# Two reorders on ScalarE and VectorE, and four large weight copies issued three tiles apart instead of at one place

## The chip, the cores and the metric

The kernel runs on one core of a Trainium2 chip. TensorE (PE in the rows) multiplies, ScalarE (ACT), VectorE (DVE) and GpSimd (POOL) do the rest, and SyncE (SP) issues most of the DMAs; GpSimd issues some. Each engine works through its own queue in order and waits on semaphores. The metric is the device time of one execution in microseconds (us). It was 1953.87 us, the median of 3 runs (1952.58 to 1955.76). A difference of under 0.2%, some 3.9 us, is about what a measurement can't tell from none.

## The reference, cut to what matters

One decoder layer for 1024 tokens and 16 meta tokens, width 1024, in float32:

```
proj = rmsnorm(h) @ w_in                      # 80 blocks of 128 columns, and 16 gate columns
gq, gk, gv = silu(causal_dwconv(...))         # 4 taps
y_a = gated_delta(gq, gk, gv, ...)            # chunked recurrence, 8 heads
y_b = retention(rotary(rq), rotary(rk), rv)   # chunked recurrence, 4 heads
h = h + (sigmoid(gate_a) * y_a + sigmoid(gate_b) * y_b) @ w_out
u = causal_dwconv(rmsnorm(h) @ w_ffn_up, 3 taps) + bias
a, b = split(u)
h = h + (silu(a) * b) @ w_ffn_down
out = rmsnorm(h)
```

## The kernel before, in words

All large products are made of three matrix products each: an operand x is split into a rounded high part and a remainder, and PE sums high x high, high x low and low x high. ACT makes the high part of a weight block (`split_high`, L1550), DVE the low part (`split_low`, L1941).

**The plan.** Up to the end of the input projection, every engine walks the same list of steps, which `front_plan` writes. A tile t is a block of 128 columns of `w_in`, and it is computed in three thirds (t, 0), (t, 1), (t, 2) of its some 1040 rows (step `proj`, L1171). Two banks of PSUM take turns, so PE starts a third only when ACT has copied out the third before the last one (`evac`, ACT L1625). The weights of tile t+2 are loaded when tile t+1 has been split (step `load`, L844), and split beside tile t+1. Tiles 0 to 15 are the rotary ones: DVE rotates a pair of tiles (`rope`, L2006 to L2016), SP stores it. Tiles 15 and 16 are computed in one piece (`proj3`, L155). Beside tile 15, ACT and DVE write the input anew, scaled by its norm, into `xh` and `xl` (ACT L1635, DVE L2028, 8 blocks each). Tile 17 needs its own low part in `w_lo`, which stands in DVE's queue behind the rope of tiles 14 and 15. Tiles 16 to 23 and 32 to 47 go through a convolution on DVE (step `conv`, L2049 and L2053) and then SiLU on ACT (step `silu`, L1684). Between the thirds stand the steps of the two recurrences. `dec` (DVE L2163, L2166) and `dec_e` (ACT L1724, L1726: two exponentials) prepare the decay factors of a chunk. The list writes SiLU of tile 46 after the third (47, 1). From tile 48 on the helper `fill` adds the thirds. A table of ACT's functions is loaded (ACT_TABLE_LOAD) whenever SiLU, exponential or sigmoid follow each other.

**The four weight copies.** For the last product (`w_ffn_down`) sums of its quarters are needed. GpSimd copies four quarters, 2816 KB each, from memory to memory as the starting values of these sums (L2589, queue q0), when tile 4 is done; later it adds to them by DMA.

**The up projection.** The first three column pairs of `w_ffn_up` are done plainly. The other 19 (pair i, i = 0 to 18, j = i + 3) are each made of seven products of half size, in PE's order 0 to 6 (pair 0 in another order), L1470. Products 0, 1, 2 and 3 go into four regions of PSUM, which are then reused: product 4 adds to the region of product 0, product 5 to that of product 2, product 6 to that of product 3. DVE's `combine(i, n)` for n = 0 to 4 (L2425, L2427, L2429, L2431, L2433) puts the regions together. PE starts product 5 of pair i only after `combine(i, 1)`, which reads product 2, and product 6 only after `combine(i, 2)`, which reads product 3. Between these, DVE does for pair j-1 the convolution (`taps`, L2361), the product with the SiLU (`gate_product`, L2367) and sums for the last product (`act_sums`: one operation up to j-1 = 10, three from 11 on, L2377 to L2383). For pair i+1 it makes four sums of weights (`quarter_sum`, L2332) and seven low parts (`quarter_split`, L2338), whose high parts ACT makes (L1789).

**Names in the rows.** `post` are the seven row buffers; `w_raw`, `w_hi`, `w_lo` a block of weights and its parts; `up_*` the same for the up projection; `u_one`, `u_two`, `u_three` the results in the combining.

Of the kernel before, what the change touches and what calls it, by code (L numbers as in the profile page):

```python
# [178 lines left out]
def front_plan():  # L179

    plan = []
    add = plan.append
# [8 lines left out]
    def unit(t, j):  # L191
        add(("proj", t, j))
        if j == 0 and not T_RV - 1 <= t < T_Q - 1 and t != T_ZB - 1:
            add(("split", t + 1))
        for n in splits_at.get((t, j), ()):
            add(("split", n))
# [26 lines left out]
    steps = {u: [] for u in range(96)}  # L223
# [11 lines left out]
    u = 34  # L235
    for b in range(NBATCH):
# [3 lines left out]
        j = 0  # L240
        while j < B32 - 1:
            u += 1
            n = min(B32 - 1 - j, 2 if u < 49 or u % 2 else 3)
# [21 lines left out]
    steps[91] += [("dl_k", 0), ("expand", 0)]  # L265
    steps[92] += [("dec", 0), ("dec_e", 0), ("qk", 0), ("dl_g", 1), ("dl_m", 1), ("dl_x", 1)]
    steps[93] += [("dl_a", 1)]
    steps[94] += [("dec", 1), ("dec_e", 1)]
    steps[95] += [("tk", 0), ("expand", 1), ("dl_x", 2)]

    def conv_tile(t):
        return T_K <= t < T_RV or T_Q <= t < T_ZB

    for u in range(96):
        t, j = T_K + u // 3, u % 3
        if t > T_K:
            unit(t, j)
        elif j == 0:
            add(("split", t + 1))
            add(("proj3", t))  # L280
            weights(t, 0)
            add(("rturn", 7))
        if j == 1 and conv_tile(t - 1):
            add(("silu", t - 1))
        if u in (90, 93):
            weights(t, j)
            add(("vstore", t - 2))
        for step in sorted(steps[u], key=lambda step: step[0] in ("tin", "tout")):
            add(step)
        if u in (92, 95):  # L290
            add(("split", T_ZB + u // 95))
        if j == 2 and (T_K <= t - 1 < T_RV or T_V <= t - 1):
            add(("vturn" if T_V <= t - 1 else "kturn", t - 1))
            if u not in (89, 92):
                add(("vstore" if T_V <= t - 1 else "kstore", t - 1))
        if t > T_K and u not in (90, 93):
            weights(t, j)
        if not conv_tile(t):
            add(("rvstore", 3 * t + j))
        elif j == 2:  # L300
            add(("conv", t))
# [4 lines left out]
    def fill():  # L306
        due, early = list(splits), list(ahead)
        splits.clear()
        ahead.clear()
        while held:  # L310
            add(held.pop(0))
        while gates:
            add(("gate", gates[-1]))
            splits.append(gates.pop())
        for n in early:
            add(("oload", n))
        t, j = units.pop(0)
        add(("proj", t, j))
        if j == 0:
            held.extend((*((("split", t + 1),) if t > T_ZB else ()), ("load", t + 2)))  # L320
        for n in due:
            if n >= 8:
                add(("ysplit", n))
            if n < 15:
                ahead.append(n + 1)
        if j == 2 and (t - T_ZB) % 2:
            add(("sig", (t - T_ZB) // 2))
            gates.append((t - T_ZB) // 2)

    fill()  # L330
    fill()
    add(("silu", T_ZB - 1))
    add(("vturn", T_ZB - 1))
# [6 lines left out]
    for c in range(NCH):  # L340
        n, nn = c + 1 < NCH, c + 2 < NCH
# [77 lines left out]
def program(nc, io, sc, out):  # L419

    with ExitStack() as ctx:
# [10 lines left out]
        def sem(name):  # L432
            return ctx.enter_context(nc.semaphore("f1_" + name))
# [113 lines left out]
        def w_parts(t):  # L547
# [4 lines left out]
            if 6 <= n < 8:  # L552
# [30 lines left out]
               for n in range(2)]  # L583
# [7 lines left out]
        w_hi, w_lo, units_done, evac, pe_x15 = (sem(n) for n in (  # L591
            "w_hi", "w_lo", "units_done", "evac", "pe_x15"))
# [16 lines left out]
        d_dec, a_dec, a_eg, w_sums, pe_qk, d_attn, pe_lev, d_q5, d_x5, d_t6, a_q6, d_x6 = (  # L609
            sem(n) for n in ("d_dec", "a_dec", "a_eg", "w_sums", "pe_qk", "d_attn", "pe_lev", "d_q5", "d_x5", "d_t6",  # L610
                             "a_q6", "d_x6"))
# [177 lines left out]
        def tiles_done(t):  # L789
            return 3 * t + 3  # L790
# [1144 lines left out]
        def _(dve):  # L1935
# [25 lines left out]
            for step in plan:  # L1961
                kind, a = step[0], step[1:]
# [32 lines left out]
                elif kind == "rope":  # L1995
                    i = a[0]
# [33 lines left out]
                elif kind == "rturn":  # L2030
                    i = a[0]
# [5 lines left out]
                elif kind == "conv":  # L2037
                    t = a[0]
                    q = convs_before(t)
                    tile = t - T_K + 8 if t < T_RV else t - T_Q if t < T_V else t - T_V + 16  # L2040
                    n = T - FRONT
# [126 lines left out]
                elif kind == "qk":  # L2168
                    c = a[0]
                    dve.wait_ge(a_dec, c + 1)  # L2170
                    for g in range(2):
                        dve.wait_ge(pe_qk, 2 * c + g + 1)
                        into = at[c % 2][seen(c), heads(g), seen(c)]
# [7 lines left out]
                elif kind == "l5r":  # L2181
                    c = a[0]
                    dve.wait_ge(pe_lev, lev(c, 2))
                    for n in range(2):
                        for odd in range(2):
                            of = 64 * odd + B32 * n
# [15 lines left out]
                elif kind == "kturn":  # L2202
                    t = a[0]
                    n = t - T_K
# [7 lines left out]
                elif kind == "vturn":  # L2212
                    t = a[0]
                    n = t - T_V
# [72 lines left out]
                elif kind == "gate":  # L2287
                    n = a[0]
# [75 lines left out]
            def gate_product(j):  # L2364
                dve.wait_ge(silu, j + 1)
                dve.wait_ge(conv, 4 * j + 4)
                dve.tensor_tensor(acc_of(j, 0), acc_of(j, 0), acc_of(j, 1), ALU.mult).then_inc(prod, 1)  # L2367
# [44 lines left out]
            def combine(i, n):  # L2412

                j = J0 + i
                left, right = slice(0, H2), slice(H2, 2 * H2)
                one, two, three = (x[:, :] for x in (u_one, u_two, u_three))
                dve.wait_ge(pe_p, max(made(i, m) for m in ((0, 1), (1, 2), (1, 2, 3), (5,), (6,))[n]))
                if n in (1, 2, 3, 4):
                    dve.wait_ge(comb, 5 * i + (None, 1, 2, 1, 1)[n])
                if n > 1:  # L2420
                    dve.wait_ge(conv, 4 * (j - 1) + (None, None, 4, 2, 4)[n])
                    dve.wait_ge(tap0, 2 * (j - 1) + (None, None, 2, 1, 2)[n])
                if n == 0:
                    dve.wait_ge(c11, 2 * i + 1)
                    ins = dve.tensor_tensor(two, region(i, 1), one, ALU.subtract)  # L2425
                elif n == 1:
                    ins = dve.tensor_tensor(three, two, region(i, 2), ALU.subtract)  # L2427
                elif n == 2:
                    ins = dve.tensor_tensor(u_out[1][:, right], three, region(i, 3), ALU.subtract)  # L2429
                elif n == 3:  # L2430
                    ins = dve.tensor_tensor(u_out[0][:, right], region(i, 2), two, ALU.subtract)  # L2431
                else:
                    ins = dve.tensor_tensor(u_out[1][:, left], two, region(i, 3), ALU.subtract)  # L2433
                ins.then_inc(comb, 1)
# [50 lines left out]
            for i in range(NPAIR):  # L2485
                j, more = J0 + i, i + 1 < NPAIR
                if i:
                    combine(i - 1, 4)
                    taps(j - 1, 0)
                    taps(j - 1, 1)  # L2490
                    combine(i, 0)
                    gate_product(j - 1)
                    act_sums(j - 1)
                if more:
                    quarter_sum(i + 1, 0)
                    quarter_sum(i + 1, 1)
                if i:
                    combine(i, 1)
                if more:
                    quarter_sum(i + 1, 2)  # L2500
                    quarter_sum(i + 1, 3)
                    quarter_split(i + 1, 0)
                    quarter_split(i + 1, 1)
                if i == 0:
                    gate_product(J0 - 1)
                    act_sums(J0 - 1)
                if not more:
                    for q in range(DEARLY):
                        down_low(q)
                if i:  # L2510
                    combine(i, 2)
                if more:
                    for n in range(2, 6):
                        quarter_split(i + 1, n)
                combine(i, 3)
                if more:
                    quarter_split(i + 1, 6)
# [57 lines left out]
        def _(pool):  # L2575
            pool.memset(zero, 0.0).then_inc(zero_set, 1)
            wd, rows = io["w_ffn_down"][0], KH * P
            a11, a12, a21, a22 = (wd[rows * k:rows * k + rows, 512 * m:512 * m + 512] for m in range(2) for k in range(2))
            ws = [sc["ws"][n].rearrange("k p c -> (k p) c") for n in range(4)]
# [3 lines left out]

            for step in plan:
                kind, a = step[0], step[1:]
                if kind == "proj" and a == (5, 0):
                    pool.wait_ge(units_done, tiles_done(4))
                    for into, of in zip(ws, (a21, a11, a11, a12)):
                        pool.dma_start(into, of).then_inc(w_sums, 16)  # L2589
                elif kind == "proj" and a[0] >= T_ZA and (3 * (a[0] - T_ZA) + a[1]) % 2 and 3 * (a[0] - T_ZA) + a[1] < 4 * KH:  # L2590
                    k = (3 * (a[0] - T_ZA) + a[1]) // 2
                    pool.wait_ge(units_done, 3 * a[0] + a[1])
                    pool.wait_ge(w_sums, 64)
                    n, k, of = (0, k, a22) if k < KH else (2, k - KH, a21)
                    add_block(n, k, of[k * P:k * P + P, :])
# [84 lines left out]
            for j in range(FT):  # L2680
# [3 lines left out]
                n, k = (1, 3)[j // KH], j % KH  # L2684
# [88 lines left out]
```

## Time and profile before

| What | Value |
|---|---|
| Median of 3 runs | 1953.87 us |
| Profiled execution: its own time, its span | 1952.47 us, 1950.7 us |
| PE busy | 1926.2 us (99%), 13173 matmuls |
| PE weight loads busy | 1859.4 us (95%) |
| DVE, ACT, POOL busy | 1283.4 us (66%), 795.9 us (41%), 328.8 us (17%) |
| DMA | 315.99 MB, mean 162 GB/s |
| Chain that ended last | PE 90%, DVE 5% |

By stages (from the span's start):

| Stage | us | PE busy | PE clock | DMA share |
|---|---|---|---|---|
| tiles 0 to 16 | 0 to 207 | 197.47 of 207 | 1.00 | 0.68 |
| tiles 17 to 47, retention | 207 to 687 | 479.74 of 480 | 1.00 | 0.59 |
| turn from tile 47 to tile 49 | 687 to 705 | 12.96 of 18 | 0.91 | 0.80 |
| rest of the input projection, gated delta, start of w_out | 705 to 1210 | 504.60 of 505 | 1.00 | 0.52 |
| w_out, first plain pairs | 1210 to 1341 | 131.00 of 131 | 1.00 | 0.29 |
| up projection in seven products | 1341 to 1727 | 383.88 of 386 | 1.00 | 0.44 |
| down projection | 1727 to 1951 | 216.56 of 224 | 0.99 | 0.65 |

PE is busy nearly throughout, so a time is lost or won only where PE stands still or its clock is lower. Idle time of the others costs nothing by itself. PE clock 1.00 is full speed (2.4 GHz), 0.50 is half of it (1.2 GHz).

### The profile page before, as it was taken

The page shows a single profiled execution, that of the slowest core. Times are in us where ns is not written, and L with a number is a line of the kernel's source. Part 1 is how long each engine was busy: PE and PEld are TensorE (multiplying, and loading weights), DVE is VectorE, ACT ScalarE, POOL GpSimd, SP SyncE. Part 2 cuts the span into 40 slices and gives each one's busy share as a digit, 9 for nine tenths or more (in the row PEclk, how much of TensorE's full clock was granted, in tenths as well). Part 3 has the DMA queues.
Part 4 walks back from the last instruction along what each step waited for, and adds up shares of the span by engine and source line. Part 5 has one row for each costly group of instructions (what it writes and reads, how often), then busy time and mean ns, then how long its engine had stood idle before and what let it go on. Part 6 is the DMA issues. An engine that isn't in the chain of part 4 may idle for free.

```text
span 1950.7 us, 32138 instructions
## 1 busy us (share of the span) xinstructions
PE 1926.2 (99%) x13173; PEld 1859.4 (95%) x13173; DVE 1283.4 (66%) x1612; ACT 795.9 (41%) x1094; POOL 328.8 (17%) x327
## 2 busy tenths in 40 slices
PE   8999999999999989999999999999999999999998
PEld 7999997999999989999999999999999999988887
DVE  6456764647676767667644434379988889877656
ACT  5223432534333445445443333235444344445443
POOL 0000002566573122212201010200000000000001
PEclk9999999999999999999999999999999999999999
DMA  9665566654455675555535552312433545578554
GB/s 296 227 203 140 129 167 190 201 181 161 156 185 141 155 179 175 164 162 153 166 108 158 157 155 77 106 68 82 131 100 109 152 152 162 152 259 280 192 191 158
DMA packets 301222, 315.99 MB, mean 162 GB/s; under 512 B 151004, under 2 KB 221124, under 8 KB 300948
## 3 DMA queue, kind: packets, MB, share of 16 engines
q1 hardware_dynamic: 291860, 290.86, 47.9%
q0 software_dynamic: 9216, 23.07, 5.8%
q8 instruction: 105, 1.72, 0.4%
q14 instruction: 41, 0.34, 0.0%
HBM read 222.76 MB, written 114.18 MB: 173 GB/s over the span
## 4 chain that ended last, share of the span: by engine, by line
PE 90%; DVE 5%; issue 1%; ACT 1%; DMA 1%; POOL 1%; DVEq 0%; SPq 0%; ACTq 0%; POOLq 0%
PE a_psum L1171 37%; PE a_psum L1470 18%; PE a_psum L1480 11%; PE a_psum L155 7%; PE a_psum L1158 5%; PE a_psum L1258 1%; PE a_psum L1277 1%; DVE post L2361 1%; PE a_psum L1255 1%; PE a_psum L1363 1%; PE a_psum L1287 1%; PE a_psum L1347 1%; PE a_psum L1378 1%; PE a_psum L1303 1%; PE a_psum L1386 1%
## 5 line engine op out<-in xcount | busy, mean ns | idle before, releaser
L1171 PE MATMUL a_psum<-xh,w_hi 128*128 128x342 f32 (+3 forms) x1632 | 529.0, 324 | 5.0 <-ACT post L1625 5.0
L1171 PE MATMUL a_psum<-xl,w_hi 128*128 128x342 f32 (+3 forms) x1632 | 523.9, 321 | 0.0
L1171 PE MATMUL a_psum<-xh,w_lo 128*128 128x342 f32 (+3 forms) x1632 | 522.0, 320 | 0.0
L1171 PEld LDWEIGHTS a_psum<-xh,w_hi 128*128 128x128 f32 x1632 | 307.7, 189 | 7.4 <-ACT post L1625 5.3
L1171 PEld LDWEIGHTS a_psum<-xl,w_hi 128*128 128x128 f32 x1632 | 307.9, 189 | 0.8
L1171 PEld LDWEIGHTS a_psum<-xh,w_lo 128*128 128x128 f32 x1632 | 307.7, 189 | 0.0
L1625 ACT ACTIVATE post<-a_psum 128x342 f32<-128x342 f32 (+3 forms) x204 | 93.2, 457 | 498.1 <-PE a_psum L1171 467.1
L1941 DVE TENSOR_TENSOR w_lo<-w_raw,w_hi 128x1024 fp32r<-128x1024 f32 x86 | 113.3, 1318 | 129.9 <-ACT w_hi L1550 129.9
L1550 ACT ACTIVATE w_hi<-w_raw 128x1024 fp32r<-128x1024 f32 x86 | 90.5, 1053 | 90.9 <-PE a_psum L155 62.6
L1480 PE MATMUL a_psum<-act_hi,down_hi 128*128 128x512 f32 (+1 forms) x324 | 124.4, 384 | 0.0
L1480 PE MATMUL a_psum<-act_hi,down_lo 128*128 128x512 f32 (+1 forms) x324 | 123.3, 381 | 0.0
L1470 PE MATMUL a_psum<-x_t_hi,up_hi 128*128 128x256 f32 x608 | 122.8, 283 | 0.3 <-DVE post L2429 0.2
L1470 PE MATMUL a_psum<-x_part_lo,up_hi 128*128 128x256 f32 x608 | 122.5, 283 | 0.0
L1480 PE MATMUL a_psum<-act_lo,down_hi 128*128 128x512 f32 (+1 forms) x324 | 122.5, 378 | 0.0
L2361 DVE SCALAR_TENSOR_TENSOR post<-post,c_par,post 128x1024 f32<-128x1024 f32 x88 | 111.2, 1282 | 2.4 <-ACT post L1826 0.6
L2053 DVE SCALAR_TENSOR_TENSOR post<-post,a_par,post 128x1040 f32<-128x1040 f32 x72 | 96.9, 1346 | 2.6
L1470 PEld LDWEIGHTS a_psum<-x_t_hi,up_hi 128*128 128x128 f32 x608 | 94.3, 190 | 0.6 <-issue 0.6
L1470 PEld LDWEIGHTS a_psum<-x_part_lo,up_hi 128*128 128x128 f32 x608 | 94.3, 189 | 0.0
L1470 PE MATMUL a_psum<-x_b_hi,up_hi 128*128 128x256 f32 x456 | 92.0, 283 | 1.9 <-DVE u_three L2427 1.7
L2582 POOL DMA_DIRECT2D down_sums<-down_sums x22 | 17.9, 814 | 444.1 <-DVE post L2367 444.1
L1470 PE MATMUL a_psum<-x_t_hi,up_sum_lo 128*128 128x256 f32 x456 | 91.8, 283 | 0.0
L1470 PE MATMUL a_psum<-x_t_lo,up_hi 128*128 128x256 f32 x456 | 91.5, 282 | 0.0
(294 smaller groups left out, 3947.3 us busy)
## 6 DMA issues: line engine op xcount, KB each, us to landing
w_raw<-in_w_in SPq DMA_DIRECT2D x75, 512.0 KB, 3.8
up_raw<-in_w_up SPq DMA_DIRECT2D x19, 1024.0 KB, 4.8
mix_scratch<-post SPq DMA_DIRECT2D x32, 522.0 KB, 3.0
down_sums<-in_w_ffn_down POOLq DMA_DIRECT2D x4, 2816.0 KB, 28.6
act_scratch<-post SPq DMA_DIRECT2D x22, 512.0 KB, 2.7
down_raw<-down_sums SPq DMA_DIRECT2D x44, 256.0 KB, 2.7
act_raw<-act_sums SPq DMA_DIRECT2D x44, 256.0 KB, 3.0
ext<-mix_scratch SPq DMA_DIRECT2D x9, 1024.0 KB, 7.2
```

The costliest lines, as they stand in the source:

```text
L155: mm = pe.matmul(psum[:, bank + j, 0:n], w[:, k, :], x[:, k, col + n * j:col + n * j + n], start=(k == 0 and part == 0), stop=(k == KC - 1 ...
L1158: mm = pe.matmul(psum[0:rows_, u % 2, n * i:n * i + n], x[:, k, x0:x0 + rows_], w, start=(k == 0 and part == 0), stop=(k == KC - 1 and par ...
L1171: mm = pe.matmul(psum[:, u % 2, 0:n], w[:, k, :], x[:, k, at0:at0 + n], start=(k == 0 and part == 0), stop=(k == KC - 1 and part == 2))
L1255: mm = pe.matmul(o, rvs[c % 2][seen(c), n, :], rsc[seen(c), h, seen(c)], start=True, stop=(c == 0))
L1258: mm = pe.matmul(o, rS[:, h, i, e * P:e * P + P], rqd[:, 2 * h + i, :], start=False, stop=(i == 1))
L1470: mm = pe.matmul(region(i, n)[:, piece], w[:, k, :], x[:, k, piece], start=(n < 4 and k == 0 and part == 0), stop=(k == 3 and part == 2), ...
L1480: mm = pe.matmul(psum[:, (0, 4, 0, 4, 0, 4, 0)[p] + m, c0:c0 + n], a, b[:, c0:c0 + n], start=(p not in (2, 5, 6) and k == 0 and part == 0) ...
L1550: act.activation(w_parts(t)[0], wr(t), ACT.Copy).then_inc(w_hi, 1)
L1625: act.activation(dst, src, ACT.Copy).then_inc(evac, 1)
L1941: dve.tensor_tensor(lo, wr(t), hi.bitcast(F32), ALU.subtract).then_inc(w_lo, 1)
L2053: dve.scalar_tensor_tensor(out=acc[:, 0:n], in0=x, scalar=w, in1=acc[:, 0:n], op0=ALU.mult, op1=ALU.add).then_inc(d_conv, 1)
L2361: dve.scalar_tensor_tensor(out=acc_of(j, s), in0=u_out[s][:, c0:c0 + SEQ], scalar=par2[:, at0:at0 + 1], in1=acc_of(j, s), op0=ALU.mult, op ...
```

## The change

It has three parts. PE and SP carry out the same instructions in the same order as before.

1. In the plan, `silu` of tile 46 stands after the third (47, 2) and not after (47, 1), and the exponentials `dec_e(1)` stand after the third (48, 0) and not before (47, 2).
2. In the up projection, `combine(i, 1)` of pairs 1 to 18 follows right behind `combine(i, 0)`, ahead of `gate_product`, `act_sums` and the first two sums of weights.
3. GpSimd issues the four copies one by one, when tiles 4, 7, 10 and 13 are done, and not all when tile 4 is done.

```diff
@@ front_plan
-    steps[94] += [("dec", 1), ("dec_e", 1)]
+    steps[94] += [("dec", 1)]
...
-        if j == 1 and conv_tile(t - 1):
+        if u == 95 or (j == 1 and u != 94 and conv_tile(t - 1)):
             add(("silu", t - 1))
...
     fill()
+    add(("dec_e", 1))
     fill()
     add(("silu", T_ZB - 1))
@@ VectorE, up projection
                     combine(i, 0)
+                    combine(i, 1)
                     gate_product(j - 1)
                     act_sums(j - 1)
                 if more:
                     quarter_sum(i + 1, 0)
                     quarter_sum(i + 1, 1)
-                if i:
-                    combine(i, 1)
@@ GpSimd
-                if kind == "proj" and a == (5, 0):
-                    pool.wait_ge(units_done, tiles_done(4))
-                    for into, of in zip(ws, (a21, a11, a11, a12)):
-                        pool.dma_start(into, of).then_inc(w_sums, 16)
+                if kind == "proj" and a[1] == 0 and a[0] in (5, 8, 11, 14):
+                    pool.wait_ge(units_done, tiles_done(a[0] - 1))
+                    n = (a[0] - 5) // 3
+                    pool.dma_start(ws[n], (a21, a11, a11, a12)[n]).then_inc(w_sums, 16)
```

ACT's queue before, from the copying out of the third (47, 0) on. The row of `post_57` is the SiLU of tile 46, the two `y` rows are `dec_e(1)`, and `w_hi` is the high part of tile 49.

```order
L1625 ACTIVATE post_55<-a_psum 128x348
L1625 ACTIVATE post_55<-a_psum 128x346
L1534 ACT_TABLE_LOAD
L1684 ACTIVATE post_57<-post_56 128x1040
L1534 ACT_TABLE_LOAD
L1724 ACTIVATE y<-y 128x1024
L1726 ACTIVATE y<-y 128x1024
L1625 ACTIVATE post_55<-a_psum 128x346
L1550 ACTIVATE w_hi<-w_raw 128x1024
L1625 ACTIVATE post_54<-a_psum 128x342 x2
L1534 ACT_TABLE_LOAD
L1684 ACTIVATE post_58<-post_56 128x1040
```

The same place in the changed kernel (its lines are one higher); the last row is followed by the SiLU of tile 47, as before.

```order
L1626 ACTIVATE post_55<-a_psum 128x348
L1626 ACTIVATE post_55<-a_psum 128x346 x2
L1535 ACT_TABLE_LOAD
L1685 ACTIVATE post_57<-post_56 128x1040
L1551 ACTIVATE w_hi<-w_raw 128x1024
L1626 ACTIVATE post_54<-a_psum 128x342
L1535 ACT_TABLE_LOAD
L1725 ACTIVATE y<-y 128x1024
L1727 ACTIVATE y<-y 128x1024
L1626 ACTIVATE post_54<-a_psum 128x342
L1535 ACT_TABLE_LOAD
```

The copying out of the third (47, 2) has moved ahead of SiLU and exponentials, and the exponentials behind that of (48, 0). The SiLU of tile 47 still stands ahead of the copying out of (48, 2).

DVE's queue before in pair 1 of the up projection, from `combine(1, 0)` to the first low part of pair 2.

```order
L2425 TENSOR_TENSOR u_two<-a_psum,u_one 128x514
L2367 TENSOR_TENSOR post_56<-post_56,post_58 128x1024
L2377 TENSOR_TENSOR act_sum_166<-post_56 128x512
L2332 TENSOR_TENSOR up_sum_106<-up_raw_104 128x512
L2332 TENSOR_TENSOR up_sum_106<-up_raw_104,up_sum_106 128x512
L2427 TENSOR_TENSOR u_three<-u_two,a_psum 128x514
L2332 TENSOR_TENSOR up_sum_106<-up_raw_104 128x512
L2332 TENSOR_TENSOR up_sum_106<-up_raw_104,up_sum_106 128x512
L2338 TENSOR_TENSOR up_raw_lo_105<-up_raw_104,up_hi_108 128x512
```

The same place in the changed kernel.

```order
L2426 TENSOR_TENSOR u_two<-a_psum,u_one 128x514
L2428 TENSOR_TENSOR u_three<-u_two,a_psum 128x514
L2368 TENSOR_TENSOR post_56<-post_56,post_58 128x1024
L2378 TENSOR_TENSOR act_sum_166<-post_56 128x512
L2333 TENSOR_TENSOR up_sum_106<-up_raw_104 128x512
L2333 TENSOR_TENSOR up_sum_106<-up_raw_104,up_sum_106 128x512
L2333 TENSOR_TENSOR up_sum_106<-up_raw_104 128x512
L2333 TENSOR_TENSOR up_sum_106<-up_raw_104,up_sum_106 128x512
L2339 TENSOR_TENSOR up_raw_lo_105<-up_raw_104,up_hi_108 128x512
```

Only the row that writes `u_three` has moved, by four or, from pair 9 on, by six rows.

## Rows read from the trace of the kernel before

**Rows 1.** Waits of PE over the whole span: who for whom, total, times, longest

```profile
PE a_psum L1171 <- ACT post L1625: 5.0, 1, 5.0
...
PE a_psum L1470 <- DVE u_three L2427: 1.7, 1, 1.7
```

**Rows 2.** PE in order of time at 695 us: start, duration, row, [idle before]

```profile
695.47 0.47 PE L1171 MATMUL a_psum<-xh,w_hi 128*128 128x342 f32 x1 [5.04 <-ACT post L1625]
```

**Rows 3.** ACT in order of time, 682 to 705 us

```profile
682.89 0.46 ACT L1625 ACTIVATE post<-a_psum 128x346 f32<-128x346 f32 x1 [1.91 <-PE a_psum L1171]
...
701.07 0.46 ACT L1625 ACTIVATE post<-a_psum 128x342 f32<-128x342 f32 x1 [4.37 <-PE a_psum L1171]
...
703.56 1.07 ACT L1684 ACTIVATE post<-post 128x1040 f32<-128x1040 f32 x1 [0.73 <-DVE post L2053]
704.85 0.46 ACT L1625 ACTIVATE post<-a_psum 128x342 f32<-128x342 f32 x1 [0.21 <-PE a_psum L1171]
```

**Rows 4.** One microsecond: busy by engine, PE's granted clock, DMA share, GB/s

```profile
696.00:697.00 1.00, 1.00 (x5) 1.00 (x5) 0.65 (x2) 0.71 (x2) 0.00 (x0) 0.50 0.29 40
```

**Rows 5.** DVE in order of time, 696 to 700 us

```profile
696.39 1.23 DVE L1941 TENSOR_TENSOR w_lo<-w_raw,w_hi 128x1024 fp32r<-128x1024 f32 x1 [0.35 <-ACT w_hi L1550]
...
699.55 3.98 DVE L2053 SCALAR_TENSOR_TENSOR post<-post,a_par,post 128x1040 f32<-128x1040 f32 x3
```

**Rows 6.** The load of tile 49's weights: its issue, and its time to landing

```profile
L844 SPq DMA_DIRECT2D w_raw<-in_w_in x1: 430/430/430, 689.1 to 689.1; - x1
...
DMA to landing us min/median/max: 3.9/3.9/3.9
```

**Rows 7.** DVE in order of time at 1380 us (pair 1 of the up projection)

```profile
1380.66 0.68 DVE L2429 TENSOR_TENSOR post<-u_three,a_psum 128x514 f32<-128x514 f32 x1
```

**Rows 8.** PE in order of time, 1381 to 1382 us: product 5, then product 6

```profile
1381.03 0.40 PE L1470 MATMUL a_psum<-x_b_hi,up_sum_lo 128*128 128x256 f32 x2
1381.48 0.48 PE L1470 MATMUL a_psum<-x_t_hi,up_hi 128*128 128x256 f32 x2
1381.80 0.40 PE L1470 MATMUL a_psum<-x_t_lo,up_hi 128*128 128x256 f32 x2
```

**Rows 9.** DVE in order of time, 1572 to 1587 us (pair 11)

```profile
1572.34 1.22 DVE L2367 TENSOR_TENSOR post<-post,post 128x1024 f32<-128x1024 f32 x1
...
1580.06 0.68 DVE L2429 TENSOR_TENSOR post<-u_three,a_psum 128x514 f32<-128x514 f32 x1
...
1586.14 0.69 DVE L2433 TENSOR_TENSOR post<-u_two,a_psum 128x514 f32<-128x514 f32 x1 [1.57 <-PE a_psum L1470]
```

**Rows 10.** PE in order of time, 1574 to 1586 us (pair 11)

```profile
1574.17 0.41 PE L1470 MATMUL a_psum<-x_t_hi,up_sum_lo 128*128 128x256 f32 x2
...
1583.08 0.41 PE L1470 MATMUL a_psum<-x_t_hi,up_hi 128*128 128x256 f32 x2
...
1585.70 0.40 PE L1470 MATMUL a_psum<-x_t_hi,up_raw_lo 128*128 128x256 f32 x2
```

**Rows 11.** ACT in order of time, 173 to 186 us

```profile
173.07 0.46 ACT L1625 ACTIVATE post<-a_psum 128x348 f32<-128x348 f32 x1 [3.36 <-PE a_psum L1171]
...
185.75 1.06 ACT L1550 ACTIVATE w_hi<-w_raw 128x1024 fp32r<-128x1024 f32 x1 [0.77 <-DMA w_raw<-in_w_in]
```

**Rows 12.** DVE in order of time, 188 to 207 us

```profile
187.99 4.71 DVE L2028 TENSOR_TENSOR xl<-y,xh 128x1044 fp32r<-128x1044 f32 x4
...
198.30 1.24 DVE L2006 TENSOR_TENSOR post<-post,ext 128x1044 f32<-128x1044 f32 x1
...
205.49 1.22 DVE L1941 TENSOR_TENSOR w_lo<-w_raw,w_hi 128x1024 fp32r<-128x1024 f32 x1
```

**Rows 13.** PE in order of time at 207 us: first matmul of tile 17

```profile
207.22 0.32 PE L1171 MATMUL a_psum<-xh,w_hi 128*128 128x348 f32 x1
```

**Rows 14.** The stretch in which the four copies run, columns as in rows 4

```profile
75.00:115.00 40.00, 40.00 (x256) 40.00 (x255) 21.37 (x18) 8.18 (x14) 0.00 (x0) 1.00 1.00 355
```

**Rows 15.** The load of a tile's weights issued at 90.7 us, amid the copies

```profile
DMA to landing us min/median/max: 10.3/10.3/10.3
```

## The prediction

> **What bounds the kernel now.** I read the page first. PE is busy 1926.2 us of a span of 1950.7 us and sits on 90% of the chain that ended last, so only its gaps and its clock can change. The waits of PE by releaser are then few. After the start, only two are over 1 us: 5.0 us for ACT's copying out of PSUM, and 1.7 us for DVE's `u_three` [rows 1]. The reader is to see that the change has two reorders and the trace two gaps. The third part, the copies, touches a stretch in which PE has no gap at all: it is busy 40.00 of 40 us beside the full DMA load [rows 14]. There it can only cost. I then followed, in order of time on each engine, what comes after each gap once it is closed; most of the working is there.
>
> **ACT's reorder.** The gap stands before third (48, 1), which waits until (47, 2) is copied out: 5.04 us until 695.47 [rows 2]. PE comes back at half clock, 0.50 (1.2 GHz) [rows 4]. The third lasts until ACT takes it at 701.07, which is 5.60 us; the next one, to 704.85, lasts 3.78 [rows 3]. So the gap costs 5.04 + 1.82 = 6.9 us in all.
>
> Now (47, 2) is copied out as soon as PE has it. PE finished (48, 0) at 695.47 - 5.04 = 690.43, so (47, 2) was ready at some 686.7, and (48, 1) runs on at 690.4 without a gap. What is late next? The SiLU of tile 46 ends at 691.0, as before, since the convolution sets it. Then ACT waits for tile 49's weights, issued at 689.09 and landed 3.9 us later, 693.0 [rows 6]. The high part (1.05) and the copying out of (48, 0) end at 694.5. Third (48, 2) needs that at 694.2: a gap of 0.3. Table load and exponentials (1.3 + 2.1) take ACT to 697.8, and (48, 1) is out at 698.2, when (49, 0) wants to start. Then the large one: ACT's next entry is the SiLU of tile 47, and behind it the copying out of (48, 2), for which (49, 1) waits. That SiLU waits for DVE, whose convolution of tile 47 ends at 699.55 + 3.98 = 703.53, and DVE's queue before it is the same. Only its 0.35 us wait for `w_hi` goes [rows 5], as `w_hi` is there at 694.1. So the convolution ends at 703.2, the SiLU (1.07) at 704.3, the copying out (0.46) at 704.7, and (49, 1) starts there. PE would be ready at 702.1, so it stands for 2.6 us in a new place. Before, (49, 1) started at 704.85 + 3.78 - 0.1 = 708.5 [rows 3]. Gain: 708.5 - 704.7 = **3.8 us**, not 6.9.
>
> It stays gained if nothing behind is tied to a fixed time. The next weights, of tile 50, are split by 712.0, and PE now wants them at 712.3. The loads of the first delta chunk follow SP's queue and end before PE's earlier start. SP's order is unchanged, so I cost these at nothing.
>
> Of the clock the rows show that a gap of 5.04 us was followed by 0.50, while after the 1.7 us gap it stayed at 1.00 (the stage table has 1.00 for 1341 to 1727). A gap of 2.6 us lies between. I take full clock, being nearer to 1.7. The Trainium skill, page "TensorE: Matmul & The Clock Gate", section Part 1 on the HAM clock gate, says that idle time of a certain length drops the array to half rate, and that activity brings it back. Whether 2.6 us is enough no row shows. If it is, the gain is 3.8 - 1.8 = 2.0 us, a rival below.
>
> **DVE's reorder.** In pair 1 PE waits for `combine(1, 1)` before product 5. Moved up, that starts at 1374.3 and the gap of 1.7 us goes. But product 6 then waits for `combine(1, 2)`. DVE works without a pause around it, and the operations ahead of it are the same ones, so it still ends at 1380.66 + 0.68 = 1381.34 [rows 7]. PE started product 6 at 1381.48 before, 0.14 after that end [rows 8], and does so now. The gap only moves by one product. Gain: **0**.
>
> From pair 2 on there is no gap before, and the move adds a wait. `combine(i, 1)` needs product 2. In pair 11 that ends at 1574.17 + 0.41 = 1574.58 [rows 10], while DVE would now reach the operation at 1572.34 [rows 9]. It idles 2.3 us, with everything in DVE's queue behind it. With the handover of 0.04 (product end 1586.10, DVE 1586.14 [rows 9, 10]) it starts at 1574.62, and `gate_product`, a step of 0.61 later, at 1575.23 and not 1572.34: 2.89 late. `combine(i, 2)` has one operation less ahead of it, so it is late by 2.89 - 0.61 = 2.28 and ends at 1580.06 + 2.28 + 0.68 = 1583.02 [rows 9]. PE starts product 6 at 1583.08 [rows 10], but needs that end 0.14 earlier. So product 6 starts at 1583.16, 0.08 late, and the restart costs a further 0.08 (its first step was 0.32 and not 0.24 after the wait in pair 1 [rows 8]): 0.16 us a pair. This holds for the nine pairs 9 to 17, in which `act_sums` has three operations. Pairs 2 to 8 have two fewer and 1.3 us of margin, and the last pair has other work there. The 1.57 us that DVE waits at the end of each pair [rows 9] takes up the rest. Cost: 9 x 0.16 = **1.4 us**. Ends: 0, if the handovers are a little shorter, and 9 x 0.29 = 2.6. The 0.29 is what the late `combine(1, 2)` cost: product 6 was due at 1381.03 + 0.24 = 1381.27, came 0.21 late, plus 0.08 for the restart [rows 8].
>
> **The copies.** The first three are free: beside the four at once, weight loads took 10.3 us [rows 15] and PE had no gap, and each is now alone. The fourth is issued after tile 13, whose last third ACT takes at 173.07 [rows 11], and shares the DMA engines with the stores of the rotated tiles 12 and 13 and with the load of tile 16's weights. That load landed at 185.75, and ACT was already waiting for it [rows 11]. From it hangs a chain: high part, eight blocks of `xh` on ACT, `xl` on DVE, the rope of tiles 14 and 15, then the low part of tile 17. DVE has 1.0 us of slack in it: eight blocks of 1.16 from 187.99 end at 197.3, and the rope starts at 198.30. The low part ends at 205.49 + 1.22 = 206.71 [rows 12], and PE starts tile 17 at 207.22 [rows 13], which leaves 0.4 after a handover of 0.1. So the load may be 1.4 us late for nothing, and each microsecond beyond is PE's. How late will it be? The copy (2816 KB), two stores (522 KB each) and the load (512 KB) are 4.48 MB. At the 355 GB/s of the full stretch [rows 14] that is 12.6 us, begun 2 us after the issue at 173.3, so all is in by 187.9: 2.2 us late. Cost: 2.2 - 1.4 = **0.8 us**. Ends: 0 if the copy is nearly through by then, and 6.6 - 1.4 = 5.2 if the load takes the 10.3 us that it took amid the four copies.
>
> The trace shows that SP's traffic got a share of the DMA engines even beside four queued copies, since that load landed at all before they were done. The Trainium skill, page "DMA: Bandwidth & Descriptors", section "Queues, rings and completion order", says that an engine takes turns between its queue rows packet by packet. With even turns, stores and load (1.6 MB) at half of 355 GB/s would take 8.8 us from the first store, be in at some 188.4, and the sum would have 1.3 in place of 0.8.
>
> **Sum.** -3.8 + 0 + 1.4 + 0.8 = -1.6 us. Against the profiled execution's own 1952.47 us that is 1950.9. The median of the runs lies 1.4 higher, at 1953.87, so I forecast a median of 1952.3, no change within 0.2% (3.9 us). One term removes time and two, by waits that were not there, give part of it back.
>
> **Rivals.**
> - *The given-back parts are free.* DVE's handover is just in time and the load less than 1.4 us late. Then -3.8 stays: 1950.1. For it: the margins are tenths. Against: both sums come out beyond them. Half of this case would measure faster by over 0.2%.
> - *The clock falls in the new gap.* Before (49, 1) PE stands 2.6 us. If the clock is then 0.50 as after the 5.04 us, 1.8 is lost again: 1952.3 + 1.8 = 1954.1. For it: after a 5.04 us gap it fell; against: after 1.7 us it didn't.
> - *The fourth copy stops PE at tile 17: slower.* The load of tile 16's weights takes 10.3 us. PE stands 5.2 us before tile 17, and such a gap brings the half clock with it, another 1.8. That is -3.8 + 1.4 + 7.0 = +4.6: 1958.5. It decides from a landing 5.1 us after issue on (3.7 + 1.4), and turns the sign of the whole from some 7 us on. For it: the two stores and the load follow the copy in the same pattern as at 87 to 91 us. Against: one copy has only 8 us of transfer, most of it before the load.
> - *Both gaps go whole.* Nothing is late next, and only the fourth copy costs: -6.9 - 1.9 + 0.8: 1943.9. Against it stand the convolution's end and the end of `combine(1, 2)`, which no part of the change moves.
>
> **How the numbers follow.** Forecast 0.58, its own range 1950.3 to 1954.5. Given-back parts free 0.18; clock 0.10; slower by the copy 0.09; both gaps gone 0.05. Faster by over 0.2%: 0.09 of the second, 0.05 of the last and 0.03 of the forecast, 0.17. Slower by over 0.2%: 0.07 of the copy's case and 0.02 of the others, 0.09. The rest, 0.74, is the same. The range, 1949.3 to 1956.8, holds all but the two outer cases and takes in an upper end of DVE's cost with a lost clock.
>
> **What would show it.** PE's waits should no longer name 5.0 us before (48, 1), but some 2.6 us before (49, 1), again for ACT's L1625 (one line higher), and no row at 0.50. In pair 1 product 6 starts as late as before against the pair's start. DVE waits some 2.2 us for PE at `u_three` in nearly all pairs, and the nine late pairs last 0.16 us longer. Tile 17 starts after a wait for `w_lo` of under 1 us. I am wrong if (49, 1) starts with no gap, if pairs 9 to 17 last as long as the others, or if the load of tile 16 lands beyond 188.5.

## The result, and the profile after

The changed kernel takes 1960.57 us (median of 6 runs, 1959.36 to 1964.86), against 1954.12 us (6 runs) before on the same chip: ratio 1.0037, 95% interval 1.0026 to 1.0048. It is 0.4% slower, outside the forecast range. Its profiled execution took 1960.2 us with a span of 1958.3 us, 7.6 us more span than before.

The waits of PE over the whole span, as in [rows 1] (who for whom, total, times, longest; lines from about 330 to 2500 are one higher now):

```profile
PE a_psum L1172 <- DVE w_lo L1942: 6.5, 2, 3.7
PE a_psum L1172 <- ACT post L1626: 2.7, 2, 2.3
PE a_psum L1471 <- DVE post L2430: 2.2, 1, 2.2
```

The 5.04 us before (48, 1) are gone. New is the first row: two stops for the low part of the weights, which did not exist before. PE in order of time shows where:

```profile
165.21 0.66 PE L1172 MATMUL a_psum<-xh,w_hi 128*128 128x348 f32 x1 [3.67 <-DVE w_lo L1942]
...
216.50 0.43 PE L1172 MATMUL a_psum<-xh,w_hi 128*128 128x348 f32 x1 [2.85 <-DVE w_lo L1942]
...
714.05 0.43 PE L1172 MATMUL a_psum<-xh,w_hi 128*128 128x342 f32 x1 [2.31 <-ACT post L1626]
...
1387.40 0.48 PE L1471 MATMUL a_psum<-x_t_hi,up_hi 128*128 128x256 f32 x2 [2.24 <-DVE post L2430]
```

The second row answers to [rows 13], the third to [rows 2] and the last to [rows 8]. The first stands before tile 13, a place that the prediction held free of any wait. How much each place is worth is read by holding the same instruction in both traces against each other:

| Same instruction | before | after | behind by | of this place |
|---|---|---|---|---|
| copying out of (13, 0), ACT | 165.45 | 171.72 | 6.27 | +6.3, tile 13 |
| copying out of (17, 0), ACT | 211.25 | 220.63 | 9.38 | +3.1, tile 17 |
| copying out of (49, 2), ACT | 716.15 | 721.90 | 5.75 | -3.6, ScalarE's part |
| combine(1, 0), DVE | 1373.66 | 1379.38 | 5.72 | |
| combine(2, 0), DVE | 1390.70 | 1396.61 | 5.91 | +0.2, pair 1 |
| combine(9, 0), DVE | 1531.43 | 1537.32 | 5.89 | 0, pairs 2 to 8 |
| combine(18, 0), DVE | 1712.79 | 1720.77 | 7.98 | +2.1, pairs 9 to 17 |
| end of the span | 1950.7 | 1958.3 | 7.6 | -0.4, rest |

Until (12, 2), which PE finished at 165.21 - 3.67 = 161.54, the two run level (before, ACT took it at 161.62). The two reorders together come to -1.3 in their own places, and -1.7 with the rest of the span; the forecast had -2.4. The copies, forecast at +0.8, come to +9.4.

**Why tile 13's weights were late.** SyncE's queue in order of time (start, time that the issue took). First the kernel before, where 16 turned stores go out one behind the other and the load follows at once:

```profile
139.90 0.33 SPq L810 DMA_DIRECT2D rkt_scratch<-ext  x1
140.28 0.56 SPq L812 DMA_DIRECT2D rkt_scratch<-ext  x1
140.88 0.49 SPq L810 DMA_DIRECT2D rkt_scratch<-ext  x1
141.41 0.56 SPq L812 DMA_DIRECT2D rkt_scratch<-ext  x1
...
149.58 0.49 SPq L844 DMA_DIRECT2D w_raw<-in_w_in  x1
```

The same stretch of the changed kernel, in which GpSimd issued its third copy at 138.94:

```profile
139.85 0.33 SPq L811 DMA_DIRECT2D rkt_scratch<-ext  x1
140.23 0.56 SPq L813 DMA_DIRECT2D rkt_scratch<-ext  x1
140.83 0.63 SPq L811 DMA_DIRECT2D rkt_scratch<-ext  x1
141.50 6.88 SPq L813 DMA_DIRECT2D rkt_scratch<-ext  x1
148.43 0.98 SPq L811 DMA_DIRECT2D rkt_scratch<-ext  x1
149.45 2.69 SPq L813 DMA_DIRECT2D rkt_scratch<-ext  x1
...
157.85 0.49 SPq L845 DMA_DIRECT2D w_raw<-in_w_in  x1
```

The issue of a 2 KB store, 0.56 us in this stretch before, takes 6.88 and then 2.69 us. The queue stands, and the load behind it goes out 8.3 us later. It then lands after 5.0 us, not much over the 3.9 of before. ACT waits for it (the second row is the one of tile 16, as in [rows 11]):

```profile
162.84 1.06 ACT L1551 ACTIVATE w_hi<-w_raw 128x1024 fp32r<-128x1024 f32 x1 [8.10 <-DMA w_raw<-in_w_in]
...
196.56 1.06 ACT L1551 ACTIVATE w_hi<-w_raw 128x1024 fp32r<-128x1024 f32 x1 [5.31 <-DMA w_raw<-in_w_in]
```

PE stands for 3.67 us and comes back at half clock (0.50, 1.2 GHz), as it did after the 5.04 us of [rows 4]; the rest of the 6.3 us is that. After the 2.85 us before tile 17 it stays at full clock (columns as in [rows 4]):

```profile
168.00:170.00 2.00, 2.00 (x8) 2.00 (x8) 0.00 (x0) 0.00 (x0) 0.00 (x0) 0.50 0.86 143
...
216.00:218.00 2.00, 1.50 (x9) 1.50 (x10) 2.00 (x4) 0.43 (x1) 0.00 (x0) 1.00 0.92 310
```

### The profile page after: what moved, and what is told of

The parts are those of the page before. It is cut to its first block, busy times and chain, and to the rows that moved or that the text cites. A ratio compares the mean times of both kernels' runs of the same rounds, so it can differ in the third digit from the quotient of the medians.

```text
span 1958.3 us, 32138 instructions
## 1 busy us (share of the span) xinstructions
PE 1929.8 (99%) x13173; PEld 1861.3 (95%) x13173; DVE 1287.3 (66%) x1612; ACT 791.0 (40%) x1094; POOL 331.1 (17%) x327
## 4 chain that ended last, share of the span: by engine, by line
PE 90%; DVE 5%; issue 1%; DMA 1%; ACT 1%; SPq 1%; DVEq 0%; ACTq 0%
PE a_psum L1172 35%; PE a_psum L1471 18%; PE a_psum L1481 11%; PE a_psum L155 9%; PE a_psum L1159 5%; PE a_psum L1259 1%; PE a_psum L1278 1%; PE a_psum L1256 1%; PE a_psum L1364 1%; PE a_psum L1288 1%; PE a_psum L1241 1%; PE a_psum L1348 1%; PE a_psum L1379 1%; PE a_psum L1304 1%; PE a_psum L1387 1%
## 5 line engine op out<-in xcount | busy, mean ns | idle before, releaser
L1790 ACT ACTIVATE up_hi<-up_sum 128x512 fp32r<-128x512 f32 x76 | 43.6, 621 | 133.4 <-DVE up_sum L2333 133.4
```

Source lines behind the costliest of these rows:

```text
L1790: act.activation(u_high[i % 2][:, n, :, :], quarter(i, n), ACT.Copy).then_inc(w_hi, 1)
```

## The experiments

My theory: the copies cost, by where they meet the turned stores, while the reorders together gain a little. The rivals: the spreading itself costs, or the DMA engines' bandwidth does, or the reorders do. Each ratio is to the kernel before on the same chip, with its 95% interval; the span is that of one profiled execution. The kernel before has a span of 1950.7 us, from an execution 1.6 us faster than its median, so what a place costs is read at one instruction in both traces, and not from the spans alone.

**The copies alone.** Only part three of the change.

> Only the four copies are issued three tiles apart; both reorders are undone. Theory: SyncE's queue is held up while it issues the 16 turned stores after tile 10 beside the third copy, so the load of tile 13's weights is issued some 8 us late, TensorE stops 3.7 us before tile 13 and restarts at half clock (6.3 us in all); the fourth copy makes the load of tile 16's weights land after 8.3 us instead of 3.7, which costs 3.1 before tile 17. So +9.4 us: a span of 1960.1. Rival, my forecast's view (the first three are free, the fourth costs 0.8, and the rest of the loss comes from the reorders): 1951.5.

Measured: ratio 1.0038 [1.0026, 1.0051], span 1958.7: stops of 3.37 us before tile 13 and 1.66 before tile 17. By the up projection it is 8.0 us behind. So the copies carry the whole loss; the stop before tile 17 is 1.2 us shorter than in the changed kernel, which accounts for most of the 1.4 short of 9.4.

**Both reorders alone.**

> Both reorders, the copies all at one place as before. Theory: ScalarE's part -3.7 us, with 2.3 us of waiting before (49, 1) at full clock; VectorE's part +0.2 in pair 1 and 9 x 0.20 in pairs 9 to 17; the last pair gives 0.2 back. Sum -1.8: a span of 1948.9. Rival (the reorders cost by themselves, the copies are harmless): a span above 1956.

Measured: ratio 1.0002 [0.9993, 1.0011], span 1953.7. The theory (-1.8 us, 0.9991) lies just below the interval; the rival is out. The profile has the expected waits (2.00 us before (49, 1), 2.25 in pair 1), but also 1.13 us for `rv_stage` at 416 us and, with no stop of PE in it, a stretch at 730 to 740 us in which the granted clock is 0.83 on average. The two parts were therefore run apart, further on.

**Only the third copy moved, and four copies one tile apart.** The edits are the places alone: `{5: (0, 1, 3), 11: (2,)}` and `{5: (0,), 6: (1,), 7: (2,), 8: (3,)}` (tile: copies).

> Before, with only the third copy moved to tile 11; the other three stay at tile 5 (the place of all four before). Theory: the turned stores after tile 10 meet it as before, and tile 13 is late by 6.3 us; the load of tile 16 meets no copy and tile 17 costs nothing: span 1957.0. Rival (the two losses are one chain: the fourth copy costs what it does only because the third had made all late): the same 6.3 here, but the fourth would then be free by itself. Rival (the third copy is only late because the first two are spread out): about 1951.

> Before, with the four copies spread by one tile each (tiles 5, 6, 7, 8), all landed before the first turned store is issued at 139.9 us. Theory: the place beside the turned stores costs, not the spreading: no wait for w_lo, span 1950.7, as before. Rival (each copy that starts apart holds up the weight load beside it, whatever else is stored): up to 3 us at several tiles between 6 and 10, span above 1954.

Measured, third copy: ratio 1.0019 [1.0010, 1.0028], span 1957.4, a stop of 3.24 us before tile 13 and none before tile 17. The copying out of (13, 0) and that of (17, 0) are both 5.6 us later than before (171.00 and 216.80), of which 0.5 stood already before the stop, so the place costs 5.0. The rest of the 6.7 us of span comes later, in good part with a lower clock between 735 and 745 us. The same instruction is held up:

```profile
142.34 6.90 SPq L812 DMA_DIRECT2D rkt_scratch<-ext  x1
149.28 0.44 SPq L810 DMA_DIRECT2D rkt_scratch<-ext  x1
149.76 2.58 SPq L812 DMA_DIRECT2D rkt_scratch<-ext  x1
```

One tile apart: ratio 0.9995 [0.9986, 1.0004], span 1950.2, no wait for `w_lo`. So the spreading by itself costs nothing, and one copy beside the turned stores does. That the first two copies are free in their places in the change is seen in its trace, which runs level until (12, 2).

**The third copy one tile later.** `{5: (0, 1, 3), 12: (2,)}`.

> Three copies at tile 5 and the third one at tile 12, one tile later than the one at tile 11 that cost 6.7 us of span. It is issued at about 150.5 us, when the 16 turned stores after tile 10 have just been issued, and lasts to 163 or so; the next turned stores start at 160.4. Theory (the meeting with the turned stores costs): no stop before tile 13, a short hold of SyncE at 161 to 164, at most 1 us of waiting in the tiles 14 to 17; span 1950.7 to 1952.5. Rival (any copy in the stretch of tiles 11 to 15 delays a weight load by sharing): the load issued at 149.6, which now meets the copy itself, lands after 8 us, and TensorE stops over 1 us before tile 13 or 14; span above 1954.

Measured: ratio 0.9996 [0.9986, 1.0005], span 1951.0, no stop. The copy was issued at 150.65, just behind the load (150.32), which landed after 4.2 us. It landed 15.0 us later, at some 165.7, so it meets the next turned stores with its end. Two of their issues are longer, by less than before; the third row lies behind the copy, and issues of its length (up to 1.58 us) also occur between 130 and 300 us in the kernel before:

```profile
160.95 2.57 SPq L812 DMA_DIRECT2D rkt_scratch<-ext  x1
164.03 2.68 SPq L812 DMA_DIRECT2D rkt_scratch<-ext  x1
167.22 1.35 SPq L812 DMA_DIRECT2D rkt_scratch<-ext  x1
```

The load behind them goes out 3.2 us later than before (174.37 against 171.17), and there that is free. A move of 11.1 us (139.51 to 150.65) thus turns 4.2 us of median (6.7 of span) into nothing.

**Queue or bandwidth?** The copies as in the change, but SyncE issues the load first, in three places. `turned(i)` issues the 16 stores that stood ahead of it (its definition is left out):

```diff
                     sp.dma_start(wr(t), weights_of(t)).then_inc(w_seen(t)[0], 16)
+                    if t in (13, 15, 17):
+                        turned(t // 2 - 2)
...
-                elif kind == "rturn":
...
+                elif kind == "rturn" and a[0] == 7:
+                    turned(7)
```

> The four copies three tiles apart (no reorders), but SyncE issues each load of the weights of tiles 13, 15 and 17 ahead of the turned stores that stood before it. Theory (the load is late because it stands in SyncE's queue behind stores whose issue is held up): the load of tile 13 is issued at about 145.5 us, when the buffer comes free, and not at 158; no stop before tile 13, and of the 8 us that the copies cost alone some 6 come back; the stop before tile 17 of up to 3 stays, as the load of tile 16's weights is late by sharing, not by order. Span about 1953. Rival (the DMA engines' bandwidth beside the copy is what delays the load): issued earlier it takes 10 us or more to land, and a stop of over 2 us stays before tile 13; span above 1956.

Measured: ratio 1.0039 [1.0027, 1.0052], span 1958.4. The time that I expected is missed, the mechanism is not. At tile 13 it goes as the theory said: the load goes out at 145.13, lands after 7.9 us beside the copy, and PE does not stop. The turned stores behind it are still held:

```profile
145.13 0.33 SPq L848 DMA_DIRECT2D w_raw<-in_w_in  x1
...
148.51 4.33 SPq L812 DMA_DIRECT2D rkt_scratch<-ext  x1
```

But all turned stores now come later, those after tile 12 meet the fourth copy (issued at 173.21), and the load behind them is tile 16's:

```profile
175.46 6.91 SPq L812 DMA_DIRECT2D rkt_scratch<-ext  x1
182.41 0.50 SPq L810 DMA_DIRECT2D rkt_scratch<-ext  x1
182.95 2.67 SPq L812 DMA_DIRECT2D rkt_scratch<-ext  x1
...
188.76 7.71 SPq L848 DMA_DIRECT2D w_raw<-in_w_in  x2
```

It goes out at 188.76 where before it was 182.01. PE stops 1.60 us before tile 16 and 4.63 us before tile 17, and restarts at half clock:

```profile
213.73 0.66 PE L1176 MATMUL a_psum<-xh,w_hi 128*128 128x348 f32 x1 [4.63 <-DVE w_lo L1946]
```

The same loss has moved by four tiles. Both halves of the question have a number here: sharing the DMA engines with the copy and the stores behind it makes a load land 4.0 us later (7.9 for 3.9), which tile 13 can bear; the standing queue makes it go out 8.3 us later, which it can't. The Trainium skill, "DMA: Bandwidth & Descriptors", section "Queues, rings and completion order", says that each engine alternates between the queue rows that have work, a packet at a time. The trace agrees: the load, issued 6.3 us after the copy, landed at 153.0, with the copy (issued at 138.87, landed after 14.0) and not a load's 3.9 us behind it.

**Only the fourth copy moved.** `{5: (0, 1, 2), 14: (3,)}`.

> Three copies at tile 5, only the fourth at tile 14: with no stop before tile 13, so that it is issued at 173.3 us, as the prediction had it, and not at 179.6. Theory (the load of tile 16's weights lands after 8.3 us as in the changed kernel): a stop of 2.9 us before tile 17, +3.1: span 1953.8. Rival (the prediction: the load is 2.2 us late): a stop of 0.8. Rival (SyncE's hold decides: the turned stores after tile 13 are issued from 160 to 171 and those after tile 15 from 183 on, so that the copy, 175 to 186, meets only the first few of the latter): under 1.

Measured: ratio 1.0014 [1.0005, 1.0023], span 1956.1, a stop of 2.40 us before tile 17. The load, issued at 182.67, landed after 7.8 us:

```profile
190.51 1.06 ACT L1550 ACTIVATE w_hi<-w_raw 128x1024 fp32r<-128x1024 f32 x1 [4.86 <-DMA w_raw<-in_w_in]
```

So the fourth copy costs by itself, and by sharing: the load stands ahead of the held stores (2.27 and 2.86 us). In this run PE's clock fell to 0.50 at 212 to 215 us, 1.6 us after the stop. By the copying out of (17, 0) the place costs 4.2 us (4.9 against the kernel before, of which 0.7 stood already before tile 13), where the changed kernel's 2.85 us at full clock cost 3.1.

**The reorders apart.**

> ScalarE's reorder alone. Theory: -3.6 us from tile 49 on, span 1947.1 (with a stop of 2.0 to 2.3 us before (49, 1) at full clock). Rival (the smaller stop is followed more often by a stretch of lower granted clock, as the run of both reorders showed 0.79 and 0.87 in 730 to 740 us): 1.6 is given back, span 1948.7, and a median at most 2 us below that of before.

> VectorE's reorder alone. Theory: the gap of pair 1 moves from product 5 to product 6 and grows by 0.2 us, the nine pairs 9 to 17 are 0.20 longer each, the last pair gives 0.2 back: +1.9 us, span 1952.6, and every pair before and after starts on time. Rival (my forecast): +1.4.

Measured, ScalarE's: ratio 0.9982 [0.9974, 0.9991], about -3.5 us (-5.1 to -1.8; the medians differ by 2.9); span 1948.6 with 0.83 clock at 730 to 740 us. VectorE's: ratio 1.0015 [1.0006, 1.0024], about +3.0 (1.2 to 4.7); its profile has +0.2 in pair 1 and +2.1 over pairs 9 to 17, and the same dip of the clock. Together -0.5, in line with 1.0002 for both. In the run of ScalarE's part the gain was 3.8 us at 716 us and 2.0 at 845, so the dip took some 1.8. It also stands in the runs of the third copy, of the fourth copy and of VectorE's part alone, where ScalarE's order is that of before; so it does not need the shorter stop. Whether it comes more often with it these runs can't say.

**Fixes.** In pair 1 alone, `combine(1, 1)` and `combine(1, 2)` follow `combine(1, 0)`; in all other pairs both stay where they were before:

```diff
                     combine(i, 0)
+                    if i == 1:
+                        combine(i, 1)
+                        combine(i, 2)
...
-                if i:
+                if i > 1:
                     combine(i, 1)
...
-                if i:
+                if i > 1:
                     combine(i, 2)
```

> Only pair 1 of VectorE's order changed: combine(1, 1) and combine(1, 2) right behind combine(1, 0). Theory: the whole gap of 1.7 us goes, with 0.1 for the restart: span 1948.9, c0 of pair 2 on 1.8 us earlier. Rival (the gap is VectorE's total work, not its order, and comes back before product 7 or at the start of pair 2, as product 6 showed when only combine(1, 1) moved): 1950.7.

Measured: ratio 0.9990 [0.9981, 0.9999]. From pair 3 on everything is 2.3 us earlier against the start of pair 1, 0.5 more than expected, and PE is busy 10.00 of the 10 us from 1370 to 1380, where it was busy 8.27. So the rival is out: DVE had the time, and its order was what cost, in one pair of 19.

With that, ScalarE's reorder, and the SiLU of tile 47 one third later:

> Copies at one place as before. ScalarE's reorder with the SiLU of tile 47 (and what follows from it) one projection third later, behind the copying out of (48, 2). VectorE's order as before but for pair 1, where combine(1, 1) and combine(1, 2) follow combine(1, 0). Theory: the stop before (49, 1) goes, since the copying out no longer waits for the convolution of tile 47: -3.6 - 2.2 us; in pair 1 neither product 5 nor product 6 waits: -1.8; pairs 9 to 17 take 20.15 us each as before. Sum -7.6: span 1943.1. Rival (the SiLU is then late for what reads it, and TensorE stops elsewhere for as long): -3.6 - 1.8: 1945.3.

Measured: ratio 0.9967 [0.9954, 0.9979], span 1947.6. The stop before (49, 1) is gone, but there are 1.79 us before (48, 2) and 2.08 us for `w_lo` before tile 50, and a stop of 1.48 us at 117 us that the edit does not touch. The rival is the nearer one. That stop at 117 us stands in the stretch of the four copies at once: the load issued at 103.5 us landed after 11.5 us, where the kernel before had 9.6 and no stop. So even there the copies are free only by a narrow margin, and not in every execution. Next, the SiLU back in its place:

> Copies at one place as before, ScalarE's reorder as in the change, VectorE's order changed in pair 1 alone (combine(1, 1) and combine(1, 2) behind combine(1, 0)); the SiLU of tile 47 where the change has it. Theory: both edits keep their own gains, -3.6 (ScalarE, as the changed kernel's trace has it) and -2.3 (pair 1, as when it was changed alone): span 1944.8, ratio 0.9970. Rival (the stop before (49, 1) brings a stretch of lower clock with it, as in the run of ScalarE's reorder alone): 1946.8.

Measured: 1948.31 us against 1953.98, ratio 0.9970 [0.9957, 0.9982]; -5.9 us was expected. Both versions beat the kernel before and the changed one and can't be told apart, so the later SiLU gives nothing that shows. In this run the clock fell after the stop before (49, 1), as the rival has it (first matmul 0.65 us):

```profile
706.00:707.00 1.00, 1.00 (x5) 1.00 (x5) 0.25 (x2) 0.00 (x0) 0.60 (x1) 0.50 0.84 128
...
730.00:740.00 10.00, 10.00 (x72) 9.77 (x72) 6.66 (x9) 3.11 (x6) 0.00 (x0) 0.83 0.70 235
```

## Why the prediction was wrong

**The step that failed is "The first three are free".** I argued from weight loads of 10.3 us beside four copies and no gap [rows 14, 15]. That stretch, 75 to 115 us, holds no turned store. The third copy was moved to 139 us, where 16 of them are issued, and I never laid its new place against SyncE's queue. Had I done so, the issue rows there would have shown 9.7 us of small stores with the load of tile 13's weights right behind them, on time by some 6 us (it came 9.4 late in all, and PE stood 3.7). That an issue on SyncE can stand for long also shows in the trace of before, with no copy of GpSimd's under way: a 448 KB store at the start, behind 2592 KB and the first loads, and a 2 KB one later:

```profile
12.11 21.11 SPq L836 DMA_DIRECT2D vt_scratch<-ext  x1
...
314.99 2.98 SPq L812 DMA_DIRECT2D kt_scratch<-ext  x1
```

The step cost 6.3 us instead of 0. The third copy alone shows it (5.0 us in the same place), and the one issued a tile later shows that it is the meeting.

**The fourth copy: right mechanism, wrong size.** The term was 2.2 us late less 1.4 of slack = 0.8. The load was 4.6 us late (8.3 to landing, for 3.7), less 1.4 is 3.2, against 3.1 measured. The slack held. The rate held too while the copy ran, as the windows of the changed kernel show (last two columns: DMA share, GB/s):

```profile
188.00:191.00 3.00, 3.00 (x21) 3.00 (x20) 2.71 (x5) 0.22 (x1) 0.00 (x0) 1.00 0.97 320
191.00:194.00 3.00, 3.00 (x21) 3.00 (x20) 0.00 (x0) 0.24 (x1) 0.00 (x0) 1.00 1.02 417
194.00:197.00 3.00, 3.00 (x21) 3.00 (x20) 0.00 (x0) 0.44 (x1) 0.00 (x0) 1.00 0.69 129
```

Begun 2 us after the issue at 179.60 (the 2 us were an estimate that no row gave), my 12.6 us would have ended at 194.2; the load was in at 196.6. What I left out of the bytes are the turned stores, issued from 189.5 on, right behind the load; in its last microseconds the engines are busy for 0.69 at 129 GB/s. That these stores are the missing 2.4 us is an inference; no run took them away. The rival "The fourth copy stops PE at tile 17" had this place right, with 5.2 us and a chance of 0.09, but this is the smaller loss; for tile 13 there was no rival at all.

**ScalarE's reorder: right.** -3.6 for -3.8; the stop before (49, 1) is 2.31 us for 2.6, at full clock, and 0.37 before (48, 2) for 0.3. Alone it measured -3.5. Whether it keeps the clock is not certain: the run with the best version lost it there.

**VectorE's reorder: right in kind, short in size.** Product 6 waits 2.24 us where product 5 waited 1.73 [rows 1]: +0.2 where I put 0. `combine(1, 1)` starts 0.79 us after `combine(1, 0)` (1380.17 after 1379.38), where before the next operation came after 0.61, and all behind it is later by that. Pair 9 is longer by 0.51 us and pairs 10 to 17 by 0.20 each, 2.1 in all for 1.4; pairs 2 to 8 by nothing, as forecast. DVE waits for PE at `u_three` in pair 11, for less than the 2.3 us forecast, which answers to [rows 9]:

```profile
1578.33 0.69 DVE L2426 TENSOR_TENSOR u_two<-a_psum,u_one 128x514 f32<-128x514 f32 x1
1580.90 0.69 DVE L2428 TENSOR_TENSOR u_three<-u_two,a_psum 128x514 f32<-128x514 f32 x1 [1.88 <-PE a_psum L1471]
...
1588.62 0.68 DVE L2430 TENSOR_TENSOR post<-u_three,a_psum 128x514 f32<-128x514 f32 x1
```

I said that no part of the change could move the end of `combine(1, 2)` in pair 1, which is so; that it could be moved by another two lines, for 2.3 us, I did not look for. The last rival's time is also added up wrongly: -6.9 - 1.9 + 0.8 is -8.0, which gives 1945.9 and not 1943.9.

**What stays open.** Why SyncE stands, whether for room in its queue on the DMA engines or for the small stores' completion, was not tried. In the changed kernel, with the copies alone and with the third copy alone it fell on the fourth and sixth issue, both 2 KB stores; with the load first it fell on the twelfth. In all four the long one begins 2.3 to 2.8 us after the copy's issue. Nor is it settled what makes the clock fall after one stop of 2.4 us and not after another.

## What to carry to other kernels

When a transfer is moved, lay it in its new place against what each issuing queue does there, not only against bytes: small stores ahead of a load, in one queue, make the load late by whatever slows them. A stretch in which big copies run beside big loads for nothing says nothing of one with small stores. And when a gap moves to the next product, move the next result's reader as well, in that pair alone: moving `combine(i, 1)` in all pairs cost 2.1 us in pairs where nothing had waited.

## What the runs showed of the hardware

- One issue of a 2 KB store on SyncE took 6.88 to 7.36 us beside a 2816 KB copy between two places of the chip's memory from GpSimd's queue, in four runs (the changed kernel, the copies alone, the third copy alone, the load first). In the kernel before most such issues take 0.56 us and the longest 2.98; a 448 KB store in the crowded start took 21.11 us to issue.
- That copy landed after 12.2 to 15.2 us when it went alone, where the four at once took 14.6 to 45.4.
- A 512 KB load landed after 7.1 to 8.3 us when it was issued beside one such copy, and after 3.7 to 3.9 us in the same places without one.
- The clock of PE after a stop: 1.00 after 2.31 and 2.85 us, 0.50 after 2.40 (fourth copy alone), 2.35 (best version), 3.67 and 5.04 us. The length of the stop alone does not decide between 2.3 and 2.9.
- In 6 of the 14 profiles the granted clock dips between 730 and 750 us with no stop of PE in that stretch (0.83 over 730 to 740 in four of them), with ScalarE's and VectorE's order of before as well as with the new ones.
